# First stage of a hybrid decoder step: keys weighed earlier in VectorE's step, the samples' decode moved ahead of the heads' root on GpSimd, first products waiting piece by piece

## What is computed

```
d_log = where(causal, b[t] - b[s] + ig[s], -inf)
m_t   = maximum(b + m, max(d_log))
s     = (q . k) * exp(d_log - m_t)
num   = exp(b + m - m_t) * (C . q) + s . v
h     = num / maximum(abs(nq), exp(-m_t))
C_new = decay * C + sum_s w_state[s] * v[s] k[s]
h_a   = rmsnorm(h, hn_g) * sigmoid(o_a)
```

## Time and profile before

| | us |
|---|---|
| three runs, median | 2463.51 (2461.54 to 2468.1) |
| the profiled execution, its own time | 2470.04 |
| its span in the trace | 2468.4 |
| steps 0 to 15 of the first stage (first dm mask to the last heads' squares) | 86.76 to 646 |
| busy time of PE, VectorE, ScalarE, GpSimd over the span | 2224.8, 1480.6, 973.3, 460.0 |
| mean granted TensorE clock, share of full speed | 0.957 |

### The profile page before, as it was taken

How to read it: one execution, slowest core, us unless ns; L and a number is a source line. 1 busy time by engine, 2 the same in 40 slices (tenths; PEclk the granted TensorE clock), 3 DMA queues, 4 the chain that set the end, 5 groups by cost and what they waited for, 6 DMA issues and landing times. The chain is left out here.

```text
span 2468.4 us, 33970 instructions
## 1 busy us (share of the span) xinstructions
PE 2224.8 (90%) x10675; PEld 1808.6 (73%) x10676; DVE 1480.6 (60%) x2827; ACT 973.3 (39%) x1567; POOL 460.0 (19%) x617
## 2 busy tenths in 40 slices
PE   5998979999389999998398999999999999969998
PEld 4887867778378888887376777777777777747775
DVE  4777767777525555454544457486664666835554
ACT  3434323333322222222344446375553556623332
POOL 0011145312012223232100000000000000023332
PEclk9999989999699999998698999999999999989999
DMA  6201212111533223231676677697776779733431
GB/s 200 67 35 60 79 39 93 57 42 52 168 99 111 94 94 119 94 115 44 221 279 240 231 254 284 236 332 272 282 283 226 263 266 354 290 141 140 142 137 64
DMA packets 157588, 407.03 MB, mean 165 GB/s; under 512 B 17131, under 2 KB 20643, under 8 KB 157278
## 3 DMA queue, kind: packets, MB, share of 16 engines
q1 hardware_dynamic: 135782, 337.14, 38.2%
q0 software_dynamic: 14560, 43.11, 5.2%
q10 hardware_dynamic: 7200, 26.22, 2.6%
HBM read 330.10 MB, written 84.82 MB: 168 GB/s over the span
## 5 line engine op out<-in xcount | busy, mean ns | idle before, releaser
L1915 DVE TENSOR_TENSOR w_lo<-raw,w_hi 128x2048 fp32r<-128x2048 f32 x196 | 436.1, 2287 | 73.4 <-ACT w_hi L1851 73.2
L1851 ACT ACTIVATE w_hi<-raw 128x2048 fp32r<-128x2048 f32 x196 | 360.0, 1926 | 70.5 <-DMA raw<-in_w 68.1
L200 PE MATMUL bank<-w_hi,mix_x 128*128 128x512 f32 x816 | 336.1, 412 | 56.5 <-DMA mix_x<-xT_dram 39.3
L202 PE MATMUL bank<-w_hi,mix_x 128*128 128x512 f32 x816 | 327.4, 401 | 0.0
L201 PE MATMUL bank<-w_lo,mix_x 128*128 128x512 f32 x816 | 327.0, 401 | 0.0
L1816 PE MATMUL bank<-w_hi,x_hi 128*128 128x512 f32 x784 | 310.8, 396 | 2.1 <-DVE x_lo L1907 2.1
L1817 PE MATMUL bank<-w_lo,x_hi 128*128 128x512 f32 x784 | 310.5, 396 | 0.0
L1818 PE MATMUL bank<-w_hi,x_lo 128*128 128x512 f32 x784 | 310.5, 396 | 0.0
L200 PEld LDWEIGHTS bank<-w_hi,mix_x 128*128 128x128 f32 x816 | 159.3, 195 | 90.1 <-DMA mix_x<-xT_dram 34.5
L202 PEld LDWEIGHTS bank<-w_hi,mix_x 128*128 128x128 f32 x816 | 158.7, 194 | 35.4
L201 PEld LDWEIGHTS bank<-w_lo,mix_x 128*128 128x128 f32 x816 | 159.3, 195 | 31.6
(11 more groups left out here) (286 smaller groups left out, 4036.4 us busy)
## 6 DMA issues: line engine op xcount, KB each, us to landing
raw<-in_w SPq DMA_DIRECT2D x96, 2048.0 KB, 11.8
y_dram<-y_sb ACTq DMA_DIRECT2D x50, 512.0 KB
xT_dram<-mix_x SPq DMA_DIRECT2D x34, 512.0 KB, 3.3
mix_x<-xT_dram SPq DMA_DIRECT2D x34, 512.0 KB, 4.1
raw_all<-in_w_in SPq DMA_DIRECT2D x24, 512.0 KB, 5.9
x_sb<-in_x_prompt SPq DMA_DIRECT2D x16, 512.0 KB
xr_sb<-in_x_prompt SPq DMA_DIRECT2D x16, 512.0 KB
h_dram<-h_sb SPq DMA_DIRECT2D x16, 512.0 KB
```

Source lines behind the costliest of these rows:

```text
L200: pe.matmul(bank[:, :], x_hi[:, k, :], wh[:, k, :], start=(k == 0), stop=False)
L202: ins = pe.matmul(bank[:, :], x_lo[:, k, :], wh[:, k, :], start=False, stop=(k == KD - 1))
L1851: return act.activation(out, in_, ACT.Copy)
L1915: dve.tensor_tensor(w_lo[slot(j, m)][:, cols], raw[m][:, cols], w_hi[slot(j, m)][:, cols].bitcast(F32), ALU.subtract).then_inc(lo_ready, 1)
```

## The change

It has three parts.

1. **The start.** gmix_b's load has a semaphore of its own, `gmix_loaded`, and VectorE's first multiply waits for that alone. ScalarE and VectorE split the eight pieces of q and k before they turn to the gates' columns. `project` takes a piece number for tile 0 and then waits for one piece (six matmuls) at a time, before every second k; PE makes q's product before it transposes the conv's weights.
2. **VectorE's step.** `weigh_keys` stands right behind the conv of q's half, ahead of the gate sums and the silu.
3. **GpSimd's step.** The heads' root of step t-1 is taken at the start of step t, ahead of the mask on dm, and the last one behind the loop. So a hook behind step t stands ahead of that step's heads' root. The samples' conv, silu and state come one step earlier on GpSimd (behind steps 1, 3 and 5); the four quarters of C stay behind 6 to 9 and the heads behind 12, and the state no longer shares its place with the first quarter. ScalarE's gates and exps and SyncE's keep_qk come one step earlier.

```
@@ -193,10 +193,13 @@
...
 
-def project(pe, bank, s):
+def project(pe, bank, s, piece=None):
+
 
...
     for k in range(KD):
+        if piece is not None and k % 2 == 0:
+            pe.wait_ge(p_lo, piece + k // 2 + 1)
         pe.matmul(bank[:, :], x_hi[:, k, :], wh[:, k, :], start=(k == 0), stop=False)
@@ -355,7 +358,7 @@
...
             load_x(0)
-            sp_.dma_start(gmix_b[:, :], a["norm_mix_g"][0, :].partition_broadcast(P)).then_inc(prep_loaded, 16)
+            sp_.dma_start(gmix_b[:, :], a["norm_mix_g"][0, :].partition_broadcast(P)).then_inc(gmix_loaded, 16)
             for p in range(RING):
@@ -476,7 +479,7 @@
...
             load_samples()
-            chunks(step, {5: keep_qk, 7: keep_state, 8: lambda: keep_rest(1), 9: lambda: keep_rest(2), 10: keep_heads,
+            chunks(step, {4: keep_qk, 7: keep_state, 8: lambda: keep_rest(1), 9: lambda: keep_rest(2), 10: keep_heads,
                           13: keep_samples})(sp_)
@@ -506,10 +509,7 @@
...
                 pe.wait_ge(x_lo_ready, 2 * n + 2)
-                if not isinstance(n, int) or n > 0:
-                    pe.wait_ge(o_in, n)
-                else:
-                    pe.wait_ge(p_lo, PIECES)
+                pe.wait_ge(o_in, n)
                 project(pe, A, 0).then_inc(q_mm, 1)
@@ -578,7 +578,7 @@
...
                     pe.wait_ge(kw_ready, n - 1)
-                elif n == 1:
+                else:
                     pe.wait_ge(v_in, 1)
@@ -615,21 +615,20 @@
...
             x_transposes(0, NS)
-            pe.wait_ge(prep_loaded, 16 * 8)
+            pe.wait_ge(x_lo_ready, 2)
+            project(pe, A, 0, 0).then_inc(q_mm, 1)
+            pe.wait_ge(prep_loaded, 16 * 7)
             for j in range(CW + 1):
...
             ins.then_inc(prep_tp, 1)
-            project_q(0)
-            pe.wait_ge(p_lo, 2 * PIECES)
-            project_k(0)
+            project(pe, B, 1, PIECES).then_inc(k_mm, 1)
             pe.wait_ge(wg_lo_ready, 1)
...
             pe.wait_ge(prep_in, 1)
-            pe.wait_ge(p_lo, 3 * PIECES)
-            project_v(0)
-            pe.wait_ge(p_lo, 4 * PIECES)
-            project_o(0)
+            project(pe, SS, 2, 2 * PIECES).then_inc(v_mm, 1)
+            pe.wait_ge(qtok_in, 1)
+            project(pe, A, 3, 3 * PIECES).then_inc(o_mm, 1)
             project_q(1)
@@ -740,10 +739,10 @@
...
             x_halves(0, NS)
-            act.wait_ge(prep_loaded, 16 * 8)
-            copy(wg_hi[:, 0:2 * KD * H], wg[:, :, :, :].rearrange("p w k h -> p (w k h)")).then_inc(wg_hi_ready, 1)
             for p in range(2 * PIECES):
                 split_hi(act, p)
+            act.wait_ge(prep_loaded, 16 * 7)
+            copy(wg_hi[:, 0:2 * KD * H], wg[:, :, :, :].rearrange("p w k h -> p (w k h)")).then_inc(wg_hi_ready, 1)
             act.wait_ge(prep_tp, 1)
@@ -788,7 +787,7 @@
...
 
-            chunks(step, {3: sample_gates, 5: sample_exps, 11: sample_squares})(act)
+            chunks(step, {2: sample_gates, 4: sample_exps, 11: sample_squares})(act)
             act.wait_ge(tail_steps, 1)
@@ -958,9 +957,10 @@
...
                     conv(t + 1, 0, sp_st)
+                weigh_keys(t)
+                if more:
                     gate_sums(t + 1, sp_st)
                     silu(t + 1, 0)
-                weigh_keys(t)
                 update(t, st)
@@ -976,14 +976,17 @@
...
             dve.wait_ge(dve_const, DVE_CONSTS)
-            dve.wait_ge(prep_loaded, 16 * 8)
+            dve.wait_ge(gmix_loaded, 16)
             norm_x(0, NS)
             x_rest(0, NS)
+            for p in range(2 * PIECES):
+                split_lo(dve, p)
+            dve.wait_ge(prep_loaded, 16 * 7)
             dve.wait_ge(wg_hi_ready, 1)
...
             TS(hng_b[:, :], hng_b[:, :], 0.5, None, ALU.mult).then_inc(dve_const, 1)
-            for p in range(4 * PIECES):
+            for p in range(2 * PIECES, 4 * PIECES):
                 split_lo(dve, p)
@@ -1037,12 +1040,16 @@
...
 
+            def rstd_heads(t):
+                rstd(pool, P, 24, 28, H, P, hh_sq, t + 1, hh_rstd, pool_steps, t)
+
             def step(t):
+                if not isinstance(t, int) or t > 0:
+                    rstd_heads(t - 1)
                 hold(pool, dm_exp, t + 1)
...
                     rstd_x(t + 3)
-                rstd(pool, P, 24, 28, H, P, hh_sq, t + 1, hh_rstd, pool_steps, t)
 
@@ -1155,12 +1162,9 @@
...
 
-            def sample_first():
-                sample_state()
-                sample_c(0)
-
-            chunks(step, {2: sample_conv, 4: sample_silu, 6: sample_first, 7: lambda: sample_c(1), 8: lambda: sample_c(2),
-                          9: lambda: sample_c(3), 12: sample_heads})(pool)
+            chunks(step, {1: sample_conv, 3: sample_silu, 5: sample_state, 6: lambda: sample_c(0), 7: lambda: sample_c(1),
+                          8: lambda: sample_c(2), 9: lambda: sample_c(3), 12: sample_heads})(pool)
+            rstd_heads(NT - 1)
 
...
     nc.all_engine_barrier()

```

41 lines of the change are left out of this document (19 added, 22 removed).

## The result

The changed kernel takes 2448.71 us (median of 5 runs, 2443.67 to 2452.67) against 2463.65 (5 runs, 2461.54 to 2468.1): ratio 0.9936, 95% interval 0.9918 to 0.9954, 15 us faster. The forecast was 35.5 us faster, 2428, and the time lies outside its range of 2408 to 2446. The profiled execution took 2450.82 us (span 2449.2).

The account below looks back on a forecast made before the run. TensorE (PE) sets the pace: its work plus idle gaps plus the lower clock's cost. Terms -10 -10.5 -15.5 -1.5 +2 = -35.5 off the median 2463.51 give 2428 us, range 2408 to 2446.

Parts of the forecast that it names:

- The start, -10: Kernel's start: VectorE's first multiply no longer waits for eight small loads; -10 us, bounds -6 to -12.5.
- The 3.29 us of ScalarE's wait for q's product: Kernel's start: ScalarE's wait before piece 8 goes as well, adding 3.3 us to the 8.3 from earlier piece issue.
- The weighed keys, -10.5: Steps 0, 2, 3, 4, 11, 13, 14: 1.5 us of kw wait goes from each; -10.5 us, poor bound -5.
- GpSimd's order, -15.5: Steps 6 to 10: the stall goes, passes stretch the conv of q's half; 178.1 against 193.6 us, bounds -19 to -5.
- The 3.9 us of steps 6 and 7: Steps 6 and 7: conv ends near 18.1, kw at 18.8, so PE, there at 14.9, waits 3.9 us.
- The clock: After longer waits for kw, PE's clock is low for some 3 us: +2 us.
- The samples' conv: Pass moved from the end of step 2 to the middle of step 1: -2 and +2 us, together 0.
- Steps 5 and 12: Small passes, state in 5 and heads in 12, operations mostly under 1 us: -1.5 us together.
- The third rival: Kernel's start is bound by the loads after all, or gmix_b lands late: -3 instead of -10, 2434.5 us; chance 0.15.
- The first (the wait only changes its name): PE, 1.5 us earlier each step, waits that long for x's low halves instead: -23.5, 2440 us; chance 0.17.
- The second: GpSimd's passes hold all of VectorE's work in front of kw; slower than before: +18, 2481 us; chance 0.04.
- The fourth: PE's stretches of low clock, 1.5 us in most steps, go with the idle gaps: another -15, 2413 us; chance 0.12.

Follow-up runs that it names:

- The early loads: Changed kernel with SyncE's load of C's third and fourth quarter issued one step earlier: 2443.15 us, ratio 0.9912.

## Why the prediction was wrong

**The start, -10: measured -6.3**, at the poor end of its bounds. The release of VectorE and ScalarE was right (10.8 and 8.15 us earlier). Wrong was the step "a piece lands 3.9 us after its issue": the first piece of the second round took 5.7. The 3.29 us of ScalarE's wait for q's product did not come on top, and tile 1 of x, for which 1.5 us had been taken off together with the clock, stopped PE for 5.4 us. Moving that tile alone brought the first mask another 6.2 us forward, 12.5 in all (3.9 to 6.2 in the three kernels that have this edit); what held the start back was mostly the place of that norm behind piece 11.

**The weighed keys, -10.5: right in its mechanism, somewhat small.** The seven plain steps are shorter by 1.74, 2.57, 4.25, 1.87, 1.82, 1.80 and 1.73 us, 15.8 together. Step 2 also lost the samples' conv. Of the 4.25 of step 3, the keys alone gave 1.06 and GpSimd's order alone 2.99: the wait of 3.1 us for x's low halves stays in the first kernel and is gone in the second, with ScalarE's gates of the samples, which the forecast put at nothing. In step 2 they bring 3.1 us in place of the conv's 2.2; so the two steps together lose the 2 us of wait that the forecast took off step 2, but in step 3 and in another way. Alone the edit gives 22.4 us in 15 steps. The forecast had it nowhere as a whole, because it counted the pass steps under GpSimd's order.

**GpSimd's order, -15.5: the term that failed.** Steps 6 to 10 were put at 178.1 us against 193.6 and took 194.88. The stall did go, as read from the earlier trace rows, but these five steps lie beyond even the poor bound of the term, -5. Start and keys without the third part gave 29.8 us; the forecast for the same (10 + 10.5, and the kw wait of 1.56 us that the 15.5 contains for each of steps 6 to 10, 7.8) was 28.3. The rest of the term, a gain of 7.7 us, measured as a cost of 13. So the miss lies in this part: in the price of the passes at their new place, in three points.
- "In steps 8 and 9 ... most of the conv runs beside the pass's multiply by a column and is held little, and PE waits about 1." The pass started 7.2 us into the step, near the 8 named, but the conv's 12 operations started 12.2 us into it, and not at 9.1 as in the earlier trace rows; by then the multiply by a column had just ended, and two large tensor_tensors followed. Of these 3.1 us, 1.6 had passed before sp (370.50, 6.1 us into the step; 4.5 in step 10), and the rest came between sp and the 12, where GpSimd was already at work. The waits were 6.22 and 6.27 us. The early loads took 2 us from each, which shows that the place within the conv made these 2 us; the other 4 are the price that steps 6 and 7 have too.
- The 3.9 us of steps 6 and 7 were 4.18 and 5.14: short by 0.3 and 1.2.
- The clock: "+2" for the whole change stood against 10.9 us in these four steps alone (141.09 against 130.22 us of PE with and without the arithmetic on C). Behind each of the four waits the matmuls run at the lower clock at once, for 2.7 to 5.7 us. The "some 3 us" of the forecast were read too short as well: behind the wait of step 7 in the trace before, PE's 128x512 matmuls stand 0.43 us apart instead of 0.23 until 368.4, 5.7 us from its start at 362.66.

Forecast for steps 6 to 9 were 144.4 us, measured 163.09, a miss of 18.7: 12.0 in waits (21.8 against 9.8) and 6.7 in the clock (10.9 against some 4 contained in the forecast, whose 33.6 us for a step without waits are 32.6 without the arithmetic on C). The separate +2 for the clock is not counted in the 144.4. In the traces the second stage starts 21.7 us earlier and not 35.5, so 13.8 us are missing in the first stage: 18.7 in these steps, 3.7 at the start and 4.0 in step 1, less 5.3 in the plain steps, 4.1 in steps 5, 10 and 12, the 2 for the clock and 1.3 behind the last mask. The other 6.8 of the 20.6 us between 2428 and 2448.7 lie in the stages behind (2.5) and in how far each profiled execution lies from its median (4.3); no edit touches either.

**The other terms.** The samples' conv was put at 0, +2 in step 1 and -2 in step 2, and gave +4.04 in step 1; step 2 has -2.57, most of it the keys' gain, and the other 2 us show in step 3, as said. Steps 5 and 12 gave -3.7 instead of -1.5; they contain the keys' gain, which the term left out. The range's upper end, 2446, added the poor bounds of the four gains without the +2 of the clock that the sum has; with it the end would be 2448. The third rival's 28.5 us give 2435.0, not 2434.5.

**The rivals.** The first (the wait only changes its name) is out: with the keys alone, x's low halves cost 2.8 us more and kw 26.8 less. The second's mechanism, GpSimd's passes on the work in front of kw, is what happened, at 3.9 to 6.3 us in five of the eight passes, short of the 6 us in each of the eight from which it was to decide. With GpSimd's order alone (7.5 to 9.1 us in steps 6 to 9) that point was passed in four of the eight passes, and the kernel was slower than before by 25 us. The rule of the Trainium skill on which it leant (page "SBUF — State Buffer", section "Who interferes with whom") fits the two gate sums of 2.60 and 2.41 us, each ending within 0.3 us of a GpSimd tensor_tensor that had started just before it. The rival's chance of 0.04 was fair for its full price; what the cases lacked was the same mechanism at 38% of it (25.7 of 68 us of waits). The third is half right: the start fell short, by less and mostly not for the loads. The fourth is out: the mean clock of steps 0 to 5 is 0.96 after 0.97.

**What was named as a sign.** "Waits for kw near 16 us" were 25.7; "kw waits of over 6 us" show in steps 8 and 9, and steps 6 to 9, at 38.4 to 42.8 us, are beyond the 34 to 38 foretold. No wait for sp but the last step's, and low halves under 20 us, held.

## What to carry to other kernels

A pass that is moved on a side engine is to be priced at its new place by what the main engine's feeder runs beside it, operation by operation and with the times of that step, not with the phases of an undisturbed one; here the conv came 3 us later than in an undisturbed step, and two large operations fell on it instead of ahead of it. A saved stall is no gain as such: here the order that removed an idle of 7 us once put waits of 4 to 6 us into five steps. Where work must contend, gate its contending part on an event behind which the other engine has slack (here the state's update), and leave the part that contends little where the slack is small (cut so, steps 6 to 9 took 141.0 us, with the whole pass behind the keys 149.2); and count the lower clock behind each wait of TensorE beside the wait, here at half of it again.

## What the runs showed of the chip

Size is no shelter from GpSimd: a scan of 4 partitions x 128, 0.41 us otherwise, took 2.60 beside a GpSimd tensor_tensor of 128x1024 that ended 0.3 us before it, and a 4x128 sum 2.41 instead of 0.28. VectorE's tensor_scalar, which reads one tensor and a column of factors, isn't free of it either: four took 3.24 us instead of 1.12. The Trainium skill's page named above counts tensor_scalar among the operations that can take the shared pair in some of their forms; whether these did, no run here shows.
